# Layer 0 of a four-layer encoder trunk: transposing x before its norm is known

## The reference

```python
def rms_norm(x, g):
    xf = x.astype(jnp.float32)
    y = xf * lax.rsqrt(jnp.mean(xf * xf, axis=-1, keepdims=True) + EPS)
    return (y * g.astype(jnp.float32)).astype(x.dtype)
...
def fox_mixer(h, w_in, b_f, qn, kn):
    proj = h @ w_in
    q = rms_norm(proj[..., :D].reshape(B, S, N_HEADS, HEAD_DIM), qn)
    k = rms_norm(proj[..., D:2 * D].reshape(B, S, N_HEADS, HEAD_DIM), kn)
    v = proj[..., 2 * D:3 * D].reshape(B, S, N_HEADS, HEAD_DIM)
    log_f = jax.nn.log_sigmoid((proj[..., 3 * D:] + b_f).astype(jnp.float32))
    cum = jnp.cumsum(log_f, axis=1).transpose(0, 2, 1)
...
    for i in range(DEPTH):
        h = rms_norm(x, attn_norm[i])
        if m == 0:
            o = fox_mixer(h, w_in_a[j], b_f[j], qn_a[j], kn_a[j])
```

## Time and profile before

| | |
|---|---|
| median of 3 runs | 1322.68 us (1322.16 to 1323.43) |
| the profiled execution, its own time | 1323.36 us |
| its span, first to last instruction | 1321.6 us |
| PE, DVE, ACT, POOL busy | 98%, 77%, 66%, 35% |
| mean granted TensorE clock | 0.995 of full |
| instructions | 22029 |

### The profile page before, as it was taken

The page is one execution under the profiler, slowest core; times in us unless marked ns, Lnnn a source line. Parts: engine busy times, 40 slices in busy tenths (PEclk is TensorE's granted clock), DMA queues, the critical chain, the costliest instruction groups (busy, mean ns, idle before and its releaser), DMA issues.

```text
span 1321.6 us, 22029 instructions
## 1 busy us (share of the span) xinstructions
PE 1294.3 (98%) x6916; PEld 1093.7 (83%) x6916; DVE 1016.8 (77%) x1621; ACT 875.4 (66%) x1569; POOL 460.3 (35%) x496
## 2 busy tenths in 40 slices
PE   6999999999999999999998899999999999999998
PEld 5888888888888888888886688888888888888887
DVE  5877898955777788885588888887476888889745
ACT  6777777744667677774466867776366776777533
POOL 3741245410275225552026315552014620555300
PEclk9999999999999999999998999999999999999999
DMA  7633555565674455556551265556456435555651
GB/s 261 227 116 130 175 191 189 190 216 166 207 230 138 151 176 188 191 187 214 162 181 64 82 222 190 183 188 218 159 185 205 134 122 178 188 190 190 207 177 64
DMA packets 64603, 232.39 MB, mean 176 GB/s; under 512 B 7473, under 2 KB 7601, under 8 KB 64529
## 3 DMA queue, kind: packets, MB, share of 16 engines
q1 hardware_dynamic: 61632, 221.35, 50.8%
q0 software_dynamic: 2896, 10.08, 2.5%
HBM read 230.35 MB, written 1.05 MB: 175 GB/s over the span
## 4 chain that ended last, share of the span: by engine, by line
PE 93%; DVE 3%; POOL 2%; DMA 1%; issue 1%; ACT 1%; SPq 0%; DVEq 0%; POOLq 0%
PE bank L1437 28%; PE bank L1687 25%; PE bank L1690 12%; PE bank L1413 6%; PE bank L1415 6%; PE bank L1414 6%; PE bank L1452 5%; PE bank L1584 2%; PE bank L1423 2%; PE bank L1607 1%; PE bank L1506 1%; DMA w_raw<-weights 1%; DVE w_lo L805 1%; POOL qr L1251 0%; POOL qn L1336 0%
## 5 line engine op out<-in xcount | busy, mean ns | idle before, releaser
L805 DVE TENSOR_TENSOR w_lo<-w_raw,w_hi 128x1024 fp32r<-128x1024 f32 x418 | 544.7, 1322 | 110.0 <-ACT w_hi L460 108.5
L460 ACT ACTIVATE w_hi<-w_raw 128x1024 fp32r<-128x1024 f32 x418 | 430.1, 1053 | 140.6 <-PE bank L1437 105.2
L1687 PE MATMUL bank<-hT,w_hi 128*128 128x512 f32 x1408 | 444.9, 396 | 0.0
L1690 PEld LDWEIGHTS bank<-hT,w_lo 128*128 128x128 f32 x1408 | 264.8, 188 | 59.3
L1690 PE MATMUL bank<-hT,w_lo 128*128 128x256 f32 x1408 | 282.4, 278 | 0.0
L1398 POOL TENSOR_TENSOR gT_lo<-gate_c,gT_hi 128x256 f32 (+1 forms) x88 | 173.7, 1974 | 201.3 <-ACT gT_hi L757 201.3
L1687 PEld LDWEIGHTS bank<-hT,w_hi 128*128 128x128 f32 x1408 | 216.8, 189 | 3.9 <-issue 1.1
L1256 POOL TENSOR_SCALAR ssq<-ssq 128x1 f32<-128x1 f32 x24 | 12.9, 536 | 369.2 <-ACT tok L486 369.2
L1413 PE MATMUL bank<-w_hi,hT 128*128 128x512 f32 (+1 forms) x336 | 134.5, 400 | 3.7 <-DVE hT L859 3.2
L1415 PE MATMUL bank<-w_hi,hT 128*128 128x512 f32 (+1 forms) x336 | 130.8, 389 | 0.0
L1414 PE MATMUL bank<-w_lo,hT 128*128 128x512 f32 (+1 forms) x336 | 130.6, 389 | 0.0
(11 more groups left out here) (161 smaller groups left out, 1975.3 us busy)
## 6 DMA issues: line engine op xcount, KB each, us to landing
w_raw<-weights SPq DMA_DIRECT2D x418, 512.0 KB, 3.5
gain<-gains POOLq DMA_DIRECT2D x11, 512.0 KB, 4.3
rel<-rel_in POOLq DMA_DIRECT2D x8, 256.0 KB, 3.7
x<-x_in SPq DMA_DIRECT2D x4, 256.0 KB, 4.9
out<-x SPq DMA_DIRECT2D x4, 256.0 KB, 2.0
p_end<-p_in POOLq DMA_DIRECT2D x3, 256.0 KB, 5.1
consts<-consts_in POOLq DMA_DIRECT2D x1, 392.0 KB, 4.6
conv_sb<-conv POOLq DMA_DIRECT2D x1, 352.0 KB, 4.1
```

The lines of the kernel that those rows point to most:

```text
L460: nc.scalar.activation(w_hi[:, slot, q * HALF:(q + 1) * HALF], w_raw[:, raw, :], ACT.Copy).then_inc(hi_ready, 1)
L805: nc.vector.tensor_tensor(w_lo[:, slot, cols], w_raw[:, half(q)[0], :], w_hi[:, slot, cols].bitcast(F32), ALU.subtract).then_inc(lo_ready, 1)
L1687: nc.tensor.matmul(up_banks(L, slot)[:, side, :], w_hi[:, *at(side)], hT[:, c, :, :], start=c == 0, stop=c == KC - 1, skip_group_check=True)
L1690: last = nc.tensor.matmul(up_banks(L, slot)[:, side, 0:SEQ], w_lo[:, *at(side)], hT_hi[:, c, :], start=False, stop=c == KC - 1, skip_group ...
```

## The change

x, the gain of layer 0's first norm and the identity become one tensor in DRAM (`first_ins`) and one in SBUF (`first_in`): for each partition 8 values of gain, 128 of identity, 8 of padding, then 2048 of x, so that x begins at byte 576 and the tensors behind it start at multiples of 64 bytes as before. SP's first transfer brings gain, identity and x of tile 0, half 0 (656 columns); two transfers are gone.

PE transposes x itself, as soon as a half has landed. Layer 0's `normalise` is gone. `rstd` is applied behind the projection: as a scale in `evacuate_item` (with `rstd_sq`, which is rstd/8, for the squares) and `evacuate_v`, in `rest_v`, and for the gate, whose logits are laid out with tokens along the row, through two more transposes on PE that turn `rstd` into a row repeated for 16 heads, and five operations in `gate_in` instead of two.

```diff
@@ the tensors
+X_AT = KC + P + 8
-        x = sb("x", [P, TT, D])
+        first_in = sb("first_in", [P, X_AT + TT * D])
+        gain0, ident = first_in[:, 0:KC], first_in[:, KC:KC + P]
+        x = first_in[:, X_AT:X_AT + TT * D].rearrange("p (t d) -> p t d", t=TT)
...
-        ident = sb("ident", [P, P])
-        gain0 = sb("gain0", [P, KC])
+        rstd_sq = sb("rstd_sq", [P, 8])
@@ SP
-                    c = slice(b * 512, (b + 1) * 512)
-                    sp.dma_start(x[:, t, c], x_in[t * P:(t + 1) * P, c]).then_inc(x_landed[2 * t + b], 16)
-                if t == 0:
-                    sp.dma_start(ident[:], ident_in).then_inc(ident_landed, 16)
-                    sp.dma_start(gain0[:], gain0_in).then_inc(gain0_landed, 16)
+                    c = slice(X_AT * (t or b) + t * D + b * 512, X_AT + t * D + (b + 1) * 512)
+                    sp.dma_start(first_in[:, c], first_ins[:, c]).then_inc(x_landed[2 * t + b], 16)
@@ ACT
+            for b in range(2):
+                round_hT(0, 0, parts=(b,))
+                split_hi(0, 0, half_of(0), first=True, halves=(b,))
+            split_hi(1, 1, half_of(1), first=True)
             square(0, 0)
-            for b in range(2):
-                split_hi(0, 0, half_of(0), first=True, halves=(b,))
-                round_hT(0, 0, parts=(b,))
-            split_hi(1, 1, half_of(1), first=True)
             square(0, 1)
             split_hi(2, 2, half_of(2), first=True)
-            split_hi(3, 3, half_of(3), first=True, halves=(0,))
-            round_hT(0, 1)
-            split_hi(3, 3, half_of(3), first=True, halves=(1,))
+            for b in range(2):
+                round_hT(0, 1, parts=(b,))
+                split_hi(3, 3, half_of(3), first=True, halves=(b,))
...
-                    nc.scalar.activation(qn[:, n % 3, 0:cols], src[:, 0:cols], ACT.Copy).then_inc(raw_ready, 1)
+                    if L == 0:
+                        act.wait_ge(rstd_sq_ready, t + 1)
+                    nc.scalar.activation(qn[:, n % 3, 0:cols], src[:, 0:cols], ACT.Copy,
+                                         scale=1.0 if L else rstd[:, t:t + 1]).then_inc(raw_ready, 1)
...
-                    nc.scalar.activation(sq[:, 0:cols], src[:, 0:cols], ACT.Square, scale=HD ** -0.5).then_inc(sq_ready, 1)
+                    nc.scalar.activation(sq[:, 0:cols], src[:, 0:cols], ACT.Square,
+                                         scale=HD ** -0.5 if L else rstd_sq[:, t:t + 1]).then_inc(sq_ready, 1)
@@ DVE
-            dve.wait_ge(x_landed[0], 16)
-            dve.wait_ge(x_landed[1], 16)
-            normalise(0, 0)
-            dve.wait_ge(gain0_landed, 16)
             for b in range(2):
+                rest_hT(0, 0, parts=(b,))
                 split_lo(0, 0, half_of(0), halves=(b,))
-                rest_hT(0, 0, parts=(b,))
             split_lo(1, 1, half_of(1))
-            dve.wait_ge(x_landed[2], 16)
-            dve.wait_ge(x_landed[3], 16)
-            normalise(0, 1)
...
@@ DVE, gate_in
+                    if L == 0:
+                        dve.wait_ge(f_done, 1)
+                        own.inc(nc.vector.tensor_copy(fe[:], aux[1][0:HEADS, SEQ:2 * SEQ]))
+                        own.inc(nc.vector.tensor_scalar(fmin[:], aux[1][2 * HEADS:3 * HEADS, 0:SEQ], 0.0, None, ALU.add))
+                        own.wait()
+                        own.inc(nc.vector.tensor_tensor(fz[:], aux[1][0:HEADS, 0:SEQ], fmin[:], ALU.add))
+                        own.wait()
+                        own.inc(nc.vector.tensor_tensor(fmin[:], fz[:], fe[:], ALU.mult))
+                        own.wait()
+                        nc.vector.tensor_scalar(fz[:], fmin[:], bf[:, 0:1], None, ALU.add).then_inc(f_z, 1)
+                        return
@@ POOL
             norm_rstd(0)
+            for t in range(TT):
+                pool.wait_ge(rstd_ready, t + 1)
+                nc.gpsimd.tensor_scalar(rstd_sq[:, t:t + 1], rstd[:, t:t + 1], HD ** -0.5, 1.0, ALU.mult, ALU.mult).then_inc(rstd_sq_ready, 1)
@@ PE, transpose_tok
-                    pe.wait_ge(tok_ready, 4 * n + 2 * t + b + 1)
+                    if n:
+                        pe.wait_ge(tok_ready, 4 * (n - 1) + 2 * t + b + 1)
+                    else:
+                        pe.wait_ge(x_landed[2 * t + b], 16)
...
-                                                   tok[:, t, k * P:(k + 1) * P], ident[:])
+                                                   (tok if n else x)[:, t, k * P:(k + 1) * P], ident)
@@ PE, before the gate's matmuls
+                    if L == 0:
+                        pe.wait_ge(rstd_ready, TT)
+                        for t in range(TT):
+                            nc.tensor.transpose(aux[1][0:HEADS, SEQ + t * P:SEQ + (t + 1) * P],
+                                                       rstd[:, t:t + 1].to_broadcast([P, HEADS]), ident)
```

More of the change, by code:

```diff
@@ L160, in half_of, with trunk @@
     return lambda q: ((2 * u + q) % RAW, (2 * u + q) // RAW + 1)
-def trunk(nc, weights, x_in, p_in, gains, gain0_in, smalls, gainT_in, bf_in, conv, wf_in, rel_in, ident_in, consts_in, out):
+def trunk(nc, weights, first_ins, p_in, gains, smalls, gainT_in, bf_in, conv, wf_in, rel_in, consts_in, out):
     with ExitStack() as ctx:
@@ L319, in trunk @@
         rstd_ready = sem("rstd_ready")
+        rstd_sq_ready = sem("rstd_sq_ready")
         tok_ready = sem("tok_ready")
@@ L591, in evacuate_v @@
                     wait_block(act, L, blk, t)
-                    nc.scalar.activation(v_hi[:, t, c * 512:(c + 1) * 512], in_bank(blk, t)[:, :], ACT.Copy).then_inc(v_hi_ready, 1)
+                    nc.scalar.activation(v_hi[:, t, c * 512:(c + 1) * 512], in_bank(blk, t)[:, :], ACT.Copy,
+                                         scale=1.0 if L else rstd[:, t:t + 1]).then_inc(v_hi_ready, 1)
                 def gate_logs():
@@ L841, in normalise @@
                 dve.wait_ge(rstd_ready, 2 * n + t + 1)
-                if n:
-                    dve.wait_ge(gain_landed, 16 * n)
+                dve.wait_ge(gain_landed, 16 * n)
                 for b in range(2):
                     c = slice(b * 512, (b + 1) * 512)
-                    if n == 0:
-                        nc.vector.tensor_scalar(tok[:, t, c], x[:, t, c], rstd[:, t:t + 1], None, ALU.mult).then_inc(tok_ready, 1)
-                        continue
                     nc.vector.scalar_tensor_tensor(tok[:, t, c], x[:, t, c], rstd[:, t:t + 1], gain[:, c],
@@ L895, in norm @@
                     rest_hT(n, 1)
-            dve.wait_ge(x_landed[0], 16)
-            dve.wait_ge(x_landed[1], 16)
-            normalise(0, 0)
-            dve.wait_ge(gain0_landed, 16)
             for b in range(2):
+                rest_hT(0, 0, parts=(b,))
                 split_lo(0, 0, half_of(0), halves=(b,))
-                rest_hT(0, 0, parts=(b,))
             split_lo(1, 1, half_of(1))
-            dve.wait_ge(x_landed[2], 16)
-            dve.wait_ge(x_landed[3], 16)
-            normalise(0, 1)
             split_lo(2, 2, half_of(2))
-            split_lo(3, 3, half_of(3), halves=(0,))
-            rest_hT(0, 1)
-            split_lo(3, 3, half_of(3), halves=(1,))
+            for b in range(2):
+                rest_hT(0, 1, parts=(b,))
+                split_lo(3, 3, half_of(3), halves=(b,))
             dve.wait_ge(wf_hi_ready, 1)
@@ L988, in rest_v @@
                         cols = slice(c * 512, (c + 1) * 512)
-                        ins = nc.vector.tensor_tensor(v_lo[:, t, cols], src[:, :], v_hi[:, t, cols].bitcast(F32), ALU.subtract)
+                        if L == 0:
+                            ins = nc.vector.scalar_tensor_tensor(v_lo[:, t, cols], src[:, :], rstd[:, t:t + 1],
+                                                                 v_hi[:, t, cols].bitcast(F32), ALU.mult, ALU.subtract)
+                        else:
+                            ins = nc.vector.tensor_tensor(v_lo[:, t, cols], src[:, :], v_hi[:, t, cols].bitcast(F32), ALU.subtract)
                     else:
@@ L1505, in transpose_items @@
                         for c in range(item_place(m, i)[3]):
-                            last = nc.tensor.transpose(item_bank(m, i)[:, c * P:(c + 1) * P], qn[:, n % 3, c * P:(c + 1) * P], ident[:])
+                            last = nc.tensor.transpose(item_bank(m, i)[:, c * P:(c + 1) * P], qn[:, n % 3, c * P:(c + 1) * P], ident)
                         last.then_inc(qk_tr, 1)
@@ L1606, in transpose_p @@
                     for c in range(3):
-                        last = nc.tensor.transpose(pt_bank(h)[:, c * P:(c + 1) * P], sc(m, h)[:, c * P:(c + 1) * P], ident[:])
+                        last = nc.tensor.transpose(pt_bank(h)[:, c * P:(c + 1) * P], sc(m, h)[:, c * P:(c + 1) * P], ident)
                     last.then_inc(pt_done, 1)
@@ L1785 @@
         "weights": np.stack(units).reshape(UNITS, P, 2, HALF).transpose(0, 2, 1, 3).reshape(2 * UNITS, P, HALF),
-        "x_in": a["x"][0],
```

(4 more changed lines are left out.)

9 lines of the change are left out of this document (4 added, 5 removed).

## The result

| | before | after |
|---|---|---|
| median of 6 runs each, same chip | 1322.42 us | 1335.16 us |
| lowest to highest | 1321.69 to 1325.27 | 1332.67 to 1335.71 |
| ratio after/before, 95% interval | | 1.0091 (1.0078 to 1.0103) |

What follows compares the result with a forecast made beforehand. PE's matmuls bound the kernel, busy 1294.3 of 1321.6 us. About 2.1 us won at the start are given back at items 1 and 5, leaving 0.3: 1322.68 - 0.3 = 1322.4 us, range 1320.4 to 1324.4.

Steps and rivals of the forecast that it cites:

- The prediction's sum: Whole kernel: start's gain given back at items 1 and 5, leaving PE 0.3 us early; median 1322.4 us, chance 0.45.
- The identity at byte 32: Rival, chance 0.05: some 500 PE transposes read the misaligned identity; at 5 to 8 ns each, 1325 to 1326.5 us.
- The start: First weight half issued 0.94 us earlier, flight still 5.80, first hT part done beforehand: first matmul at 9.9, not 12.0.
- the restart: PE's restart after tile 1's transposes: reached at 17.96, restart at 23.9 instead of 25.67, 1.8 us early.
- nearly half: PE's idle time: about 27 us in all, nearly half of it in the 12.0 us before the first matmul.
- 12% more on the transfers of x: DMA of x: rows starting off 256-byte multiples cost up to 8 beats on 64, 12% on four transfers.
- (a) Squares: ACT's four squares, after the fourth weight half, end at 15.85; the second rstd comes as late as now.
- (b) rstd_sq: Two operations ahead of POOL's six loads: 0.45 us in all, bounds 0.2 and 1.3; DVE's fourth weight half over by 15.
- (c): small's landing releases POOL, then ACT; evacuations, sums and items move by +0.45 us while PE moves by -1.8.
- (d): ACT's copies with a scale per partition: 0.08 us more for each of an item's two operations; item 0's sum 0.16 later.
- (e) The gate: DVE's five operations instead of two take 2.0 us, not 0.92: +1.1 us (0.9 to 1.4), all on ACT's path.
- The waits for items 1 and 5: PE's new waits for POOL's scaled items: 0.3 us at item 1 and 0.9 us at item 5.

Runs made afterwards that it cites:

- experiment 1: Kernel before with 64 unused bytes per partition ahead of x, nothing else: 1332.46 us, ratio 1.008.
- experiment 5: Changed kernel with 56 instead of 8 values of padding, so hT and gT keep their distance to the weights modulo 256 bytes: 1324.4 us, ratio 1.0014.
- experiment 3: Kernel before with 64 unused bytes ahead of w_raw, so weights and operands move together: 1322.37 us, ratio 1.0.
- experiment 4: Kernel before with 64 unused bytes ahead of w_hi and 64 more ahead of x: 1332.98 us, ratio 1.0078.
- experiment 6: Kernel before with 192 unused bytes ahead of x: 1325.28 us, ratio 1.0026.
- experiment 7: Kernel before with 32 unused bytes ahead of x: 1334.93 us, ratio 1.0096.
- experiment 10: Kernel before with 64 unused bytes ahead of hT and 192 behind it, so hT alone moves against the weights modulo 256: 1326.19 us, ratio 1.0028.
- experiment 11: Kernel before with POOL's scaling of gainT and small put behind item 0's work and ScalarE's wait for it moved later: 1323.17 us, ratio 1.0001.
- experiment 2: Changed kernel with 24 instead of 8 values of padding, so all behind x moves by another 64 bytes: 1337.35 us, ratio 1.0117.
- experiment 8: Version of experiment 5 with POOL's two rstd_sq operations moved behind its last small load: 1322.05 us, ratio to before 0.9998.
- experiment 9: Experiment 8 with POOL's scaling of gainT and small put behind item 0's work and ScalarE's wait for it moved later: 1322.35 us, ratio 0.9998.

## Why the prediction was wrong

**The step that failed.** The prediction's sum has no term for where the operands of the unchanged matmuls lie: that "the tensors behind it start at multiples of 64 bytes as before" was taken as no change. The only address that the prediction put a price on was the identity's, at byte 32. The move of `hT` and `gT` against the weights by 64 bytes modulo 256 costs 12.0 us of pitch by the sum over the matmuls, 10.0 us by experiment 1, 10.8 us by experiment 5. No rival had it, so the range ended at 1324.4, 10.8 us under the result. The prediction read the rows of PE's matmuls for their count and clock only; that 0.227 and 0.233 us stand next to each other in before's own trace, for one shape at one clock, was there to be asked about.

**The identity at byte 32** costs nothing that the trace shows: the 116 transposes of `qn` have a median of 272 ns after and 273 before. That rival, at 5 to 8 ns each, falls.

**The start.** The first matmul was forecast for 9.9 and came at 8.79, the restart for 23.9 and came at 23.43. The first weight half, issued at 1.67, had landed by 6.42, when ACT begins on it: at most 4.8 us of flight instead of the 5.80 that the sum kept. But the start differs from one execution to the next, and the forecast read the slowest start on record. In the eight traces with the order of before (before and experiments 1, 3, 4, 6, 7, 10, 11) the first matmul comes at 10.49 to 12.00, median 10.9, and 12.00 is before's own; in the five with the order of the change (after and experiments 2, 5, 8, 9) it comes at 8.79 to 10.08, median 9.53. So 9.9 is near the usual value, and the gain there is 1.4 us by the medians and not 2.1. ACT begins on the first weight half at 6.73 to 8.43 (median 7.4) in the eight and at 6.42 to 7.71 (median 7.2) in the five: that it is issued 0.94 us earlier brings some 0.2 by the medians. The rest fits the 1.04 us of the first `hT` part, which is done before the weights land. And the waits ahead of the first matmul, 6.9 and 3.2, are 10.1 of the 27 us that PE idles, over a third and not nearly half.

The restart came near its forecast by another path. PE reached tile 1's transposes at 16.42, not 17.96; the slow matmuls in front of them ended 4.4 us after the first one, against 5.3 in before and 2.7 in experiment 5. What PE waited for then was ACT, whose squares and splits kept it from rounding `hT` until 17.50. In experiments 5, 8 and 9 the restart is at 23.72 to 23.74 whether the first matmul came at 8.97 or at 9.72. (The granted clock of before reads 1.00 from 12 to 17 us, although the matmuls there start every 0.43 us; that they run at the 1.2 GHz level is read from this pitch alone.)

The estimate by the Trainium skill's DMA: Bandwidth & Descriptors, How a descriptor splits into AXI transactions, of 12% more on the transfers of x can't be seen here: the four transfers of x land 3.0 to 6.5 us after their issue (median 4.8), before 2.6 to 7.0 (median 4.9), and the one that got longer also carries 72 KB more.

**(a) Squares** ended at 15.70, forecast 15.85: right. **(b) rstd_sq**, 0.45 us forecast with 1.3 as its bound, took 2.38. They stand beside DVE's two differences of 16.68 to 19.04: "over by 15" holds for unit 1's halves, but unit 2's follow. Each of the two ends 0.05 us after the difference beside it. In experiment 8 the first stands beside a difference and takes 1.09, again until 0.05 after its end, and the second, behind it, takes 0.18: 1.24 in all. The Trainium skill's GPSIMD Engine Reference, Specifications, names this contention, and the prediction had weighed it and taken the lower value. **(c)** POOL's loads begin 2.0 us later than before (19.03 against 17.04), yet it had `gainT` at 26.88 instead of 27.49, as `small` flew under 5.0 us instead of 7.5; in experiment 5 the flight was 5.8 and `gainT` came at 28.09. Here too before's trace is the latest of its kind: in the seven with the order of before at this place (all but experiment 11) `gainT` comes at 25.55 to 27.49, median 25.9, in after and experiments 2 and 5 at 26.88 to 28.09, median 28.05. **(d)** 0.69 us against 0.60: as forecast. **(e) The gate** took 2.8 us and not 2.0: four operations took 0.34 to 0.42, but the product `fmin<-fz,fe` took 1.07. It stands beside POOL's scaling of item 3, 46.79 to 47.83, and ends 0.27 us after it, and so it does in experiments 2, 5 and 8. In experiment 9 POOL is done at 45.04, before DVE begins, and the same product takes 0.41:

```profile
43.35 1.68 POOL L1330 TENSOR_TENSOR qn<-qn,hrstd 128x512 f32<-128x512 f32 x1
```

```profile
46.04 0.41 DVE L1003 TENSOR_TENSOR fmin<-fz,fe 16x256 f32<-16x256 f32 x1
```

**The sum.** Held against experiment 5, where the pitch is out of it, the forecast of 0.3 us gained meets 1.9 us lost. The waits for items 1 and 5 are there, 0.6 and 1.5 us instead of 0.3 and 0.9. So the mechanism of the sum was right (a gain at the start, given back at these two items), and three of its sizes were not. (b) was 1.9 too small; in the trace `small`'s flight, 5.8 instead of 7.5, hides most of that, and that `gainT` came at 28.09 where the forecast had 27.9 is luck. (e) was 0.8 too small; POOL ends item 5 at 64.74 and not 63.75, and that is most of this 1.0. And the gain at the start was counted from a late start, while the forecast for the median took it off a usual one. What (b) is worth is shown by experiment 8: with it out of the way 2.3 us come back, and the time is 1322.05. In the kernel after itself the second of the two waits is 0.6 us and the first is missing: the landing of `small` was early in that execution.

**Best version.** Experiment 8 and 9, at 1322.05 and 1322.35, can't be told from the kernel before (1322.47 and 1322.64 beside them). None beats it.

**What stays open.** Why the pitch depends on the distance, and why the up projection goes the other way: it is shown that the placement of the two operands to each other sets it, in steps tried of 0, 32, 64, 128 and 192 bytes, not by what in the memory or the engine. Distances of 256 were tried only together with the change (experiment 5). The identity was not moved by itself, and no version was found in which both kinds of matmul have their lower pitch. No run was made to move the product `fmin<-fz,fe` and POOL's scaling apart by themselves; that POOL holds the product up rests on five traces.

## What to carry to other kernels

When a change adds, drops or resizes an SBUF tensor in a kernel whose TensorE is 98% busy, compare the start addresses of each matmul's two operands, modulo 256, before and after; if they moved against each other, pad them back and time that version before judging the change. Keep a padded copy of the kernel before as a control: it costs one run and separates placement from the change. And an operation put on POOL ahead of a load counts by what it takes beside DVE's work, there 1.2 us each, not by what it takes alone. Read more than one trace of the kernel before when a forecast is about a microsecond or two: its start alone varied by 1.5 us.

## What the runs showed of the hardware

- A matmul of 128x512 at the same clock (2.4 GHz; granted 1.00 in these stretches) starts every 227 or every 233 ns depending on where its stationary and moving operands lie to each other in SBUF. That is with the weights moving; in the up projection, where they are stationary, it is 233 at distance 0 and 229 at 64. Over some 5,700 matmuls that read a split weight this is 12 us of 1322.
- Moving all operands together by 64 bytes changes nothing (1322.37 against 1322.41 us).
- Two POOL operations on 128 x 1, which take 0.2 us each with DVE idle, took 2.38 us together beside two DVE differences on 128 x 1024, each ending 0.05 us after the difference beside it; in experiment 8 the first took 1.09 beside a difference and the second 0.18 behind it.
- A DVE product of two 16 x 256 tensors in SBUF took 1.07 us beside a POOL product on 128 x 512, in four traces, and 0.41 us in the one trace where POOL had finished before (experiment 9).
